# An encoder layer with expert retrieval: one-hot vectors made by ScalarE, rows moved between stages, gate loads from another queue

## The chip, the cores and the metric

The kernel runs on one core of a Trainium2 chip. The metric is the time of one execution on the device, in microseconds. Five engines work beside each other, each through its own list of instructions in order: TensorE (PE in the profile), VectorE (DVE), ScalarE (ACT), GpSimd (POOL) and SyncE (SP, which only issues transfers). They meet at semaphores. Everything is fp32.

## The reference

One layer of an encoder over 512 tokens of width 2048: a mixing part, a cross-attention into 256 memory tokens, and a feed-forward part by retrieval, each with a residual and a LayerNorm. The change touches the last part, and where its work is put beside the two others:

```
q = (xt @ w_pq).reshape(T, PEER_HEADS, PEER_QUERY)
s1 = einsum('thd,nd->thn', q[..., :PEER_HALF], sub_keys1)      # 128 keys
s2 = einsum('thd,nd->thn', q[..., PEER_HALF:], sub_keys2)      # 128 keys
v1, i1 = top_k(s1, 16);  v2, i2 = top_k(s2, 16)
top_s, pos = top_k(all 256 sums v1 + v2, 16);  idx = i1 * 128 + i2 of the chosen
gate = softmax(top_s)
act = gelu(sum over d of peer_u[idx] * x) * gate               # 8 heads x 16 experts a token
out = sum over the chosen experts of act * peer_v[idx]
```

There are 16384 experts, each one row of `peer_u` and one of `peer_v`, of 2048 numbers.

## The kernel before

The 512 tokens are four blocks of 128. Blocks 0 and 1 compute the retrieval **by rows**: for each of 128 chosen places of a token GpSimd gathers one row of `peer_u` for every token of the block (1.05 MB for 128 tokens, an indirect DMA), VectorE takes the dot product (L1898), ScalarE the GELU of four such columns, and VectorE adds the gathered row of `peer_v` times its factor (L1909). One such step for 128 tokens is called a row here; there are 256, each with two transfers of 1.05 MB. The dot product of row k + 4 is done together with the addition of row k. Blocks 2 and 3 (d in the names) compute it **densely**: all 16384 experts in 128 tiles of 128, by TensorE: `U` tiles (L1143), a GELU (L1442), a product with a matrix of gates (`weigh`, L1961), and `V` products (L1170), in four groups of 40, 32, 32 and 24 tiles. Each tile of weights is one transfer of 1 MB from SyncE, with four buffers (`SLOTS`).

The matrix of gates is made in the **one-hot stage**, beside U tiles 19 to 34. A chosen expert is a pair of key numbers. For four tokens at a time (n = 0 to 63) `one_hot_vectors(n)` on VectorE compares the key numbers of the 128 chosen places with the column numbers `IOTA`: plain vectors (is_equal, one TENSOR_TENSOR of 128x512, L1947) and vectors times the gate (four TENSOR_SCALAR, L1950). Their product on TensorE (`one_hots(n)`, L1155, four matmuls of 128x128) is the token's 128x128 matrix of gates. `OH` holds two sets. TensorE does one-hots for two n, half a U tile, two n, the other half. ScalarE copies each result from PSUM (four banks, `stage_gates(n)`) into a staging buffer `WS` for eight n; SyncE stores it to DRAM (`store_gates`), and at the next n divisible by 8 ScalarE waits for that store (`gates_out`) before it overwrites `WS`. Later the gates are loaded back by expert tile (`load_gates(q)`), into two buffers `WD`; q = 0 to 4 by SyncE, from 5 on by GpSimd.

The order of rows is written out by hand: `some_rows(n)` does n rows on VectorE at that place in its list, `HALVES_BEFORE` is how many pairs of rows are done before the V products, and `half_pos` spreads the rest evenly over the 216 positions of the dense part. In the stages of mixing and attention VectorE adds each product of TensorE to x (`add_mix`, L1802), and TensorE waits for these additions and for the norms (L1606 to L1612) behind them before it transposes the result (`turned`, L912). Rows between them on VectorE delay both.

## Time and profile before

| | |
|---|---|
| Three runs | 3187.04, 3189.92, 3194.26 us; median 3189.92 |
| Profiled execution | 3188.36 us, span 3186.5, mean granted TensorE clock 0.989 |
| TensorE busy | 3082.0 us, 97% |
| VectorE busy | 2062.2 us, 65% |
| ScalarE busy | 364.4 us, 11% |
| GpSimd busy | 696.4 us, 22% |
| DMA | 1023.44 MB, mean 321 GB/s |

The page cuts the span into 40 slices of 80 us; each digit is the busy share in tenths, and PEclk the granted clock in tenths.

```profile
PE   8999999999996999999989999999999999999997
DVE  5364633442777798999996766656566565555575
ACT  1223202311001211112210000000000000000000
PEclk9999999999997999999999999999999999999998
DMA  7222221176896698999999999999999999999995
```

TensorE is busy nearly all the time, with one deep slice, the 13th (960 to 1040 us), and VectorE is full around slices 15 to 21. The one-hot stage lies from 1449 to 1620 us, the V products begin at 1668. A share of busy time does not tell what sets the end; the waits and the order of time do.

### The profile page before, as it was taken

The page shows a single profiled execution, that of the slowest core. Times are in us where ns is not written, and L with a number is a line of the kernel's source. Part 1 is how long each engine was busy: PE and PEld are TensorE (multiplying, and loading weights), DVE is VectorE, ACT ScalarE, POOL GpSimd, SP SyncE. Part 2 cuts the span into 40 slices and gives each one's busy share as a digit, 9 for nine tenths or more (in the row PEclk, how much of TensorE's full clock was granted, in tenths as well). Part 3 has the DMA queues.
Part 4 walks back from the last instruction along what each step waited for, and adds up shares of the span by engine and source line. Part 5 has one row for each costly group of instructions (what it writes and reads, how often), then busy time and mean ns, then how long its engine had stood idle before and what let it go on. Part 6 is the DMA issues. An engine that isn't in the chain of part 4 may idle for free.

```text
span 3186.5 us, 26888 instructions
## 1 busy us (share of the span) xinstructions
PE 3082.0 (97%) x10342; PEld 1885.6 (59%) x10342; DVE 2062.2 (65%) x3070; ACT 364.4 (11%) x650; POOL 696.4 (22%) x553
## 2 busy tenths in 40 slices
PE   8999999999996999999989999999999999999997
PEld 5444444444445478679873446885448884468743
DVE  5364633442777798999996766656566565555575
ACT  1223202311001211112210000000000000000000
POOL 0000000000331143422224343223222222222230
PEclk9999999999997999999999999999999999999998
DMA  7222221176896698999999999999999999999995
GB/s 276 73 79 72 82 66 60 37 265 237 317 411 278 259 387 353 422 394 370 380 359 384 399 392 421 421 418 417 418 421 421 418 419 416 422 421 421 418 406 217
DMA packets 151655, 1023.44 MB, mean 321 GB/s; under 512 B 16368, under 2 KB 21616, under 8 KB 35568
## 3 DMA queue, kind: packets, MB, share of 16 engines
q0 software_dynamic: 78800, 559.97, 42.9%
q1 hardware_dynamic: 72736, 461.86, 37.0%
q8 instruction: 78, 1.28, 0.2%
q14 instruction: 41, 0.34, 0.0%
HBM read 1000.79 MB, written 20.97 MB: 321 GB/s over the span
## 4 chain that ended last, share of the span: by engine, by line
DMA 39%; PE 36%; DVE 18%; issue 4%; POOL 1%; ACT 1%; DVEq 0%; SPq 0%; ACTq 0%
DMA arena<-peer_v,arena 37%; PE ps L726 11%; DVE arena L1909 6%; PE ps L1170 5%; PE ps L996 3%; PE ps L1143 3%; PE ps L894 2%; PE ps L920 2%; DVE arena L1950 2%; DVE arena L1898 2%; PE ps L797 1%; DVE arena L1947 1%; DVE arena L1836 1%; DMA arena<-peer_ut 1%; PE ps L690 1%
## 5 line engine op out<-in xcount | busy, mean ns | idle before, releaser
L1170 PE MATMUL ps<-arena 128*128 128x512 f32 x2048 | 884.1, 594 | 18.4 <-DVE arena L1961 14.2
L1143 PE MATMUL ps<-arena 128*128 128x256 f32 x4096 | 892.6, 379 | 2.4 <-DMA arena<-peer_ut 2.4
L1143 PEld LDWEIGHTS ps<-arena 128*128 128x128 f32 x4096 | 774.6, 190 | 110.5 <-DMA arena<-peer_ut 4.6
L1909 DVE SCALAR_TENSOR_TENSOR arena<-arena 128x2048 f32<-128x2048 f32 x256 | 602.9, 2355 | 296.3 <-DMA arena<-peer_v,arena 229.6
L1898 DVE CUSTOM_DVE_ANT_0 arena<-arena 128x2048 f32<-128x2048 f32 x256 | 587.0, 2294 | 276.6 <-DMA arena<-peer_u,arena 275.9
L1170 PEld LDWEIGHTS ps<-arena 128*128 128x128 f32 x2048 | 390.1, 191 | 510.1 <-issue 488.4
L638 POOL DMA_INDIRECT arena<-peer_u,arena x256 | 347.5, 1357 | 1060.9 <-DVE arena L1898 864.5
L653 POOL DMA_INDIRECT arena<-peer_v,arena x256 | 325.5, 1272 | 722.9 <-DVE arena L1909 682.4
L726 PE MATMUL ps<-arena 128*128 128x512 f32 x800 | 345.2, 592 | 1.1 <-ACT arena L1210 1.1
L726 PEld LDWEIGHTS ps<-arena 128*128 128x128 f32 x800 | 151.9, 190 | 192.2 <-issue 192.2
L1210 ACT ACTIVATE arena<-ps 128x512 f32<-128x512 f32 (+2 forms) x247 | 144.5, 612 | 763.6 <-PE ps L912 147.4
L894 PE MATMUL ps<-arena 128*128 128x512 f32 x512 | 221.2, 592 | 0.0
L1424 ACT ACTIVATE arena<-arena 128x4 f32<-128x4 f32 x64 | 13.1, 205 | 1505.7 <-DVE arena L1898 1505.7
L894 PEld LDWEIGHTS ps<-arena 128*128 128x128 f32 x512 | 97.0, 190 | 120.1 <-issue 120.1
L920 PE MATMUL ps<-arena 128*128 128x512 f32 x320 | 139.4, 593 | 2.5 <-ACT arena L1210 2.5
L996 PE MATMUL ps<-arena 128*128 128x256 f32 x640 | 139.6, 380 | 1.2 <-ACT arena L1210 0.8
L996 PEld LDWEIGHTS ps<-arena 128*128 128x128 f32 x640 | 121.4, 190 | 18.5 <-DMA arena<-w_feat 1.2
L920 PEld LDWEIGHTS ps<-arena 128*128 128x128 f32 x320 | 60.5, 190 | 75.3 <-issue 71.8
L1833 DVE MAX8 arena<-arena 128x8 f32<-128x128 f32 (+1 forms) x192 | 52.1, 328 | 43.8 <-ACT arena L1210 38.2
L1674 DVE TENSOR_TENSOR arena<-arena 128x512 f32<-128x512 f32 x16 | 11.0, 689 | 99.9 <-ACT arena L1259 99.9
L1950 DVE TENSOR_SCALAR arena<-arena 128x128 f32<-128x128 f32 x256 | 74.5, 401 | 0.0
L1760 DVE TENSOR_REDUCE arena<-ps 128x1 f32<-128x512 f32 x32 | 22.1, 689 | 72.5 <-PE ps L833 72.0
(183 smaller groups left out, 1847.9 us busy)
## 6 DMA issues: line engine op xcount, KB each, us to landing
arena<-peer_ut SPq DMA_DIRECT2D x128, 1024.0 KB, 9.2
arena<-peer_vt SPq DMA_DIRECT2D x128, 1024.0 KB, 9.1
arena<-w_row SPq DMA_DIRECT2D x52, 1024.0 KB, 8.3
arena<-w_mix SPq DMA_DIRECT2D x40, 1024.0 KB, 4.9
arena<-w_once SPq DMA_DIRECT2D x74, 512.0 KB, 3.5
arena<-w_feat SPq DMA_DIRECT2D x20, 1024.0 KB, 10.0
dense_gates<-arena SPq DMA_DIRECT2D x8, 2048.0 KB, 8.6
arena<-dense_gates POOLq DMA_DIRECT2D x11, 1024.0 KB, 24.5
```

Source lines behind the costliest of these rows:

```text
L638: pool.indirect_dma_start(UB[e], None, peer_u, bass.IndirectOffsetOnAxis(ap=IDX[:, r:r + 1], axis=0)).then_inc(u_full[e], 16)
L653: pool.indirect_dma_start(VB[e], None, peer_v, bass.IndirectOffsetOnAxis(ap=IDX[:, r:r + 1], axis=0)).then_inc(v_full[e], 16)
L726: last = pe.matmul(out_ap, tile(t + half)[:, k * P:(k + 1) * P], A[:, kt * S:(kt + 1) * S], start=(kt == 0), stop=(kt == KT - 1))
L894: last = pe.matmul(bank(k), Y[:, b * D + kt * P:b * D + (kt + 1) * P], w[:, i * 512:(i + 1) * 512], start=(kt == NL), stop=(kt == NL - 1))
L920: last = pe.matmul(bank(k), XT[:, kt * P:(kt + 1) * P], w[:, i * 512:(i + 1) * 512], start=(kt == 0), stop=(kt == KT - 1))
L996: last = pe.matmul(ps[:, k + f // 2, (f % 2) * DT:(f % 2 + 1) * DT], w[:, kt * P:(kt + 1) * P], XTD[:, kt * DT:(kt + 1) * DT], start=(kt = ...
L1143: last = pe.matmul(ps[:, (e // 2) % 4, (e % 2) * DT:(e % 2 + 1) * DT], w[:, kt * P:(kt + 1) * P], XTD[:, kt * DT:(kt + 1) * DT], start=(kt ...
L1170: last = pe.matmul(bank(4 + (c % 2) * 2 + tb), G[:, t * DT + tb * P:t * DT + (tb + 1) * P], w[:, i * 512:(i + 1) * 512], start=(t == 0), s ...
L1210: return act.activation(dst, src, ACT.Copy)
L1898: dve.tensor_tensor_reduce(UB[e], UB[e], xrow(b), 1.0, 0.0, ALU.mult, ALU.add, DOT[r // 4 % 2][:, r % 4:r % 4 + 1]).then_inc(u_free, 1)
L1909: dve.scalar_tensor_tensor(out=acc, in0=VB[e], scalar=AV[r // 4 % 2][:, r % 4:r % 4 + 1], in1=acc, op0=ALU.mult, op1=ALU.add).then_inc(v_f ...
L1950: last = dve.tensor_scalar(oh[:, 0, i], IOTA, turn[:, 0, 4 * n + i:4 * n + i + 1], turn[:, 2, 4 * n + i:4 * n + i + 1], ALU.is_equal, ALU. ...
```

## The change

Five edits. (1) The plain vectors move to ScalarE: `plain_vectors(n)` makes |IOTA - key| with Abs in four ACTIVATE of 128x128 (bias is a column of `TB`), and max(0, 1 - that) with Relu in one of 128x512, which is 1 where the numbers are equal and 0 elsewhere. It uses one buffer `FAR`, and the second step waits for the first. On ScalarE, `plain_vectors(n + 1)` stands ahead of `stage_gates(n)`. TensorE waits for both kinds. (2) In the one-hot stage VectorE does 24 whole rows instead of 16, behind the vectors 1, 4 and 6 of each eight. (3) Ahead of it: twice 4 rows for 6, once 4 for 2. With the 8 more in the stage this is 6 more rows before the V products, `HALVES_BEFORE` 41 for 38. (4) The last store of gates is split, and the first load waits for its first part and the earlier stores only. (5) Gate loads 2, 3 and 4 are issued by ScalarE, between its GELUs, not by SyncE.

```diff
-HALVES_BEFORE = 38
+HALVES_BEFORE = 41
-GELU_AT = [16 * k + 8 for k in range(4)]
+HOT_ROWS = [8 * (i // 3) + (1, 4, 6)[i % 3] for i in range(24)]
+GELU_AT = [HOT_ROWS[4 * k + 3] + 1 for k in range(5)]
+        FAR = OT
 # SyncE
             def load_gates(q):
-                if q >= 2:
-                    sp.wait_ge(g_ready, q - 1)
             def store_gates(k):
                 sp.wait_ge(ws_ev, 8 * k + 8)
-                sp.dma_start(gates_d[k], WS).then_inc(gates_out, 16)
+                if k < DT // TG - 1:
+                    sp.dma_start(gates_d[k], WS).then_inc(gates_out, 16)
+                else:
+                    first = 8 * TG
+                    sp.dma_start(gates_d[k][:, 0:first], WS[:, 0:first]).then_inc(gates_first, 16)
+                    sp.dma_start(gates_d[k][:, first:], WS[:, first:]).then_inc(gates_out, 16)
...
                         if k == DT // TG - 1:
+                            sp.wait_ge(gates_first, 16)
+                            sp.wait_ge(gates_out, 16 * (DT // TG - 1))
+                            load_gates(0)
                             sp.wait_ge(gates_out, 16 * (DT // TG))
-                            load_gates(0)
                             load_gates(1)
-                if p == TILES[0] + 3:
-                    load_gates(2)
...
 # TensorE
                     pe.wait_ge(hots_ready, n + 1)
+                    pe.wait_ge(plain_ready, n + 1)
 # ScalarE
+            def plain_vectors(n):
+                if n >= 2:
+                    act.wait_ge(oh_mm, n - 1)
+                if n:
+                    act.wait_ge(plain_ready, n)
+                for i in range(4):
+                    t = DT + 4 * n + i
+                    last = act.activation(FAR[:, i * NK:(i + 1) * NK], IOTA, ACT.Abs, scale=-1.0, bias=TB[:, t:t + 1])
+                last.then_inc(far_done, 1)
+                act.wait_ge(far_done, n + 1)
+                act.activation(OH[n % 2][:, 4 * NK:8 * NK], FAR, ACT.Relu, scale=-1.0, bias=ONES[:, 0:1]
+                               ).then_inc(plain_ready, 1)
...
+            act.wait_ge(tb_ev, 1)
+            plain_vectors(0)
             for n in range(DT // 4):
+                if n + 1 < DT // 4:
+                    plain_vectors(n + 1)
                 if n % 8 == 1:
                     gelu_dense(0, t)
...
+            def load_gates(q):
+                act.wait_ge(g_ready, q - 1)
+                act.dma_start(WD[q % 2] ...).then_inc(wd_in[q % 2], 16)
...
                 for _ in range(TILES[g]):
+                    if p in (1, 2, 4):
+                        load_gates({1: 2, 2: 3, 4: 4}[p])
                     rows_until(p)
 # VectorE
-                dve.tensor_tensor(oh[:, 1], IOTA.unsqueeze(1).broadcast_to([P, 4, NK]),
-                                  turn[:, 1, here].unsqueeze(2).broadcast_to([P, 4, NK]), ALU.is_equal)
...
                 add_mix(b, 2, k, "mix231.2")
-            some_rows(6)
+            some_rows(4)
...
                 add_mix(b, 0, 6 + k, "mix31.0")
-            some_rows(6)
+            some_rows(4)
...
             best_pairs(0, 2)
-            some_rows(2)
+            some_rows(4)
...
                 one_hot_vectors(n)
-                if n % 4 == 1:
-                    row_ahead(rows[0])
-                if n % 4 == 3:
-                    row_add(rows[0])
-                    rows[0] += 1
+                if n in HOT_ROWS:
+                    some_rows(1)
```

VectorE between the additions of `mix31.0` and `mix31.1` (SCALAR_TENSOR_TENSOR with ps; ISA on 128x2048 is the dot product, the SCALAR_TENSOR_TENSOR on 128x2048 the addition of a row), before:

```order
L1909 SCALAR_TENSOR_TENSOR arena<-arena 128x2048 [waits v_free,v_full4]
L1898 ISA arena<-arena 128x2048 [waits u_full0]
L1898 ISA arena 128x1
L1909 SCALAR_TENSOR_TENSOR arena<-arena 128x2048 [waits v_free,v_full0]
L1921 TENSOR_TENSOR arena<-arena 128x4 [waits gel_done]
L1898 ISA arena<-arena 128x2048 [waits u_full1]
L1898 ISA arena 128x1
L1909 SCALAR_TENSOR_TENSOR arena<-arena 128x2048 [waits v_free,v_full1,act_done]
L1898 ISA arena<-arena 128x2048 [waits u_full0]
L1898 ISA arena 128x1
L1909 SCALAR_TENSOR_TENSOR arena<-arena 128x2048 [waits v_free,v_full0]
L1802 SCALAR_TENSOR_TENSOR arena<-arena,ps 128x512 [waits wb_used] x2
```

And after, where the block has four rows instead of six:

```order
L1938 SCALAR_TENSOR_TENSOR arena<-arena 128x2048 [waits v_free,v_full4]
L1950 TENSOR_TENSOR arena<-arena 128x4 [waits gel_done]
L1927 ISA arena<-arena 128x2048 [waits u_full1]
L1927 ISA arena 128x1
L1938 SCALAR_TENSOR_TENSOR arena<-arena 128x2048 [waits v_free,v_full0,act_done]
L1927 ISA arena<-arena 128x2048 [waits u_full0]
L1927 ISA arena 128x1
L1938 SCALAR_TENSOR_TENSOR arena<-arena 128x2048 [waits v_free,v_full1]
L1831 SCALAR_TENSOR_TENSOR arena<-arena,ps 128x512 [waits wb_used] x2
```

The two rows that stood last before the addition have gone from here; BN_STATS, the norm of block 3, follows it at once in both.

ScalarE in the one-hot stage, before (128x128x4 is the staging copy, 128x512 at L1442 the dense GELU, 128x4 the GELU of four rows):

```order
L1210 ACTIVATE arena<-ps 128x128x4 [waits v_free,u_free,oh_mm]
L1442 ACTIVATE arena<-ps 128x512 [waits wb_used]
L1210 ACTIVATE arena<-ps 128x128x4 [waits oh_mm] x7
L1424 ACTIVATE arena<-arena 128x4 [waits act_done,u_free]
L1210 ACTIVATE arena<-ps 128x128x4 [waits gates_out,oh_mm]
L1442 ACTIVATE arena<-ps 128x512 [waits wb_used]
L1210 ACTIVATE arena<-ps 128x128x4 [waits oh_mm] x7
```

And after, over the first turn of `WS` (128x128 at L1439 is Abs, 128x512 at L1442 Relu, 128x512 at L1459 the dense GELU):

```order
L1214 ACTIVATE arena<-ps 128x128x4 [waits oh_mm]
L1439 ACTIVATE arena<-arena 128x128 [waits plain_ready,oh_mm]
L1439 ACTIVATE arena<-arena 128x128 x3
L1442 ACTIVATE arena<-arena 128x512 [waits far_done]
L1214 ACTIVATE arena<-ps 128x128x4 [waits gates_out,oh_mm]
L1439 ACTIVATE arena<-arena 128x128 [waits plain_ready,oh_mm]
L1439 ACTIVATE arena<-arena 128x128 x3
L1442 ACTIVATE arena<-arena 128x512 [waits far_done]
L1459 ACTIVATE arena<-ps 128x512 [waits wb_used]
L1214 ACTIVATE arena<-ps 128x128x4 [waits oh_mm]
L1439 ACTIVATE arena<-arena 128x128 [waits plain_ready,oh_mm]
L1439 ACTIVATE arena<-arena 128x128 x3
```

Between two copies now stand five instructions and two waits of ScalarE for itself, and those for n + 2 stand behind the copy that waits for `gates_out`.

SyncE at the end of the one-hot stage, before:

```order
L538 DMA dense_gates<-arena 128x4096 [waits ws_ev]
L532 DMA arena<-dense_gates 128x8x256 [waits gates_out]
L532 DMA arena<-dense_gates 128x8x256
L488 DMA arena<-peer_ut 128x2048 [waits wb_used] x2
L488 DMA arena<-peer_vt 128x2048 [waits wb_used] x4
L532 DMA arena<-dense_gates 128x8x256 [waits g_ready]
L488 DMA arena<-peer_vt 128x2048 [waits wb_used]
L532 DMA arena<-dense_gates 128x8x256 [waits g_ready]
L488 DMA arena<-peer_vt 128x2048 [waits wb_used] x2
L532 DMA arena<-dense_gates 128x8x256 [waits g_ready]
L488 DMA arena<-peer_vt 128x2048 [waits wb_used] x33
```

And after; the three loads of gates are now in ScalarE's list:

```order
L544 DMA dense_gates<-arena 128x256 [waits ws_ev]
L545 DMA dense_gates<-arena 128x3840
L534 DMA arena<-dense_gates 128x8x256 [waits gates_out,gates_first]
L534 DMA arena<-dense_gates 128x8x256 [waits gates_out]
L492 DMA arena<-peer_ut 128x2048 [waits wb_used] x2
L492 DMA arena<-peer_vt 128x2048 [waits wb_used] x40
```

## Rows read from the trace of the kernel before

**Rows 1.** Waits of TensorE, whole span: us in total, times, longest.
```profile
PE ps L912 <- DVE arena L1802: 22.7, 1, 22.7
PE ps L1170 <- DVE arena L1961: 14.2, 3, 9.7
PE ps L912 <- DVE arena L1612: 8.6, 4, 5.9
...
PE ps L1170 <- DMA arena<-peer_vt: 4.2, 1, 4.2
```

**Rows 2.** Busy time of stretches; behind it TensorE clock, DMA share, GB/s.
```profile
982.00:993.00 11.00, 4.53 (x20) 4.13 (x20) 10.27 (x24) 2.99 (x5) 0.93 (x1) 0.50 0.98 409
1449.20:1620.00 170.80, 170.54 (x1011) 153.48 (x1010) 169.71 (x360) 40.13 (x76) 45.61 (x31) 1.00 0.96 373
1750.00:3000.00 1250.00, 1250.00 (x4310) 818.70 (x4309) 768.50 (x654) 37.44 (x88) 344.17 (x312) 1.00 1.01 416
```

**Rows 3.** Order of time, TensorE, 946 to 997: start, us, what [idle before].
```profile
946.36 13.90 PE L920 MATMUL ps<-arena 128*128 128x512 f32 x32
982.94 4.53 PE L912 MATMUL ps<-arena 128*128 128x128 f32 x20 [22.68 <-DVE arena L1802]
993.38 3.68 PE L912 MATMUL ps<-arena 128*128 128x128 f32 x16 [5.92 <-DVE arena L1612]
```

**Rows 4.** Order of time, VectorE, 896 to 983.
```profile
896.03 2.35 DVE L1909 SCALAR_TENSOR_TENSOR arena<-arena 128x2048 f32<-128x2048 f32 x1 [0.49 <-DMA arena<-peer_v,arena]
...
914.47 1.88 DVE L1802 SCALAR_TENSOR_TENSOR arena<-arena,ps 128x512 f32<-128x512 f32 x3
...
963.44 2.35 DVE L1909 SCALAR_TENSOR_TENSOR arena<-arena 128x2048 f32<-128x2048 f32 x1 [2.67 <-DMA arena<-peer_v,arena]
...
981.61 1.27 DVE L1802 SCALAR_TENSOR_TENSOR arena<-arena,ps 128x512 f32<-128x512 f32 x2
```

**Rows 5.** Order of time, VectorE (`d.prob`) and TensorE (its transposes), 1035 to 1045.
```profile
1035.59 1.23 DVE L1826 TENSOR_TENSOR arena<-arena 128x1024 f32<-128x1024 f32 x1
...
1043.62 1.04 PE L1012 MATMUL ps<-arena 128*128 128x128 f32 x8
```

**Rows 6.** Order of time, VectorE in the one-hot stage.
```profile
1490.44 0.72 DVE L1947 TENSOR_TENSOR arena<-arena 128x512 f32<-128x512 f32 x1
1491.04 1.15 DVE L1950 TENSOR_SCALAR arena<-arena 128x128 f32<-128x128 f32 x4
1492.06 2.33 DVE L1898 CUSTOM_DVE_ANT_0 arena<-arena 128x2048 f32<-128x2048 f32 x1
```

**Rows 7.** Order of time, TensorE in the one-hot stage.
```profile
1454.44 1.95 PE L1155 MATMUL ps<-arena 128*128 128x128 f32 x16
1456.22 3.62 PE L1143 MATMUL ps<-arena 128*128 128x256 f32 x16
1459.68 1.95 PE L1155 MATMUL ps<-arena 128*128 128x128 f32 x16
```

**Rows 8.** ScalarE by line and form: count, busy us, mean ns.
```profile
L1424 ACT ACT_TABLE_LOAD x14 | 18.0, 1283 | 0.3
...
L1424 ACT ACTIVATE arena<-arena 128x4 f32<-128x4 f32 x64 | 13.1, 205 | 1505.7 <-DVE arena L1898 1505.7
L1255 ACT ACTIVATE arena<-arena 128x512 f32<-128x512 f32 x16 | 10.7, 713 | 1.7 <-ACT arena L1249 1.7
```

**Rows 9.** Order of time, ScalarE, 123 to 128 and 1509 to 1519.
```profile
126.35 1.33 ACT L1255 ACTIVATE arena<-arena 128x512 f32<-128x512 f32 x2 [0.21 <-ACT arena L1249]
...
1517.93 0.60 ACT L1210 ACTIVATE arena<-ps 128x512 f32<-128x512 f32 x1 [7.35 <-DMA dense_gates<-arena]
```

**Rows 10.** Waits of all engines, 1440 to 1640.
```profile
ACT arena L1210 <- DMA dense_gates<-arena: 59.1, 7, 9.7
```

**Rows 11.** Order of time, VectorE and SyncE at the first V products.
```profile
1677.07 0.43 SPq L532 DMA_DIRECT2D arena<-dense_gates  x1
...
1704.44 2.29 DVE L1961 TENSOR_TENSOR arena<-arena 128x2048 f32<-128x2048 f32 x1 [11.73 <-DMA arena<-dense_gates]
```

More of the change, by code:

```diff
@@ L435, in build @@
         hots_ready, oh_mm = sem("hots_ready"), sem("oh_mm")
+        far_done, plain_ready = sem("far_done"), sem("plain_ready")
         ws_ev, gates_out = sem("ws_ev"), sem("gates_out")
+        gates_first = sem("gates_first")
         wd_in = [sem(f"wd_in{e}") for e in range(2)]
@@ L1467, in _ @@
             gelu_rows()
-            gelu_rows()
             pq(0, 2)
@@ L1475, in _ @@
             did(evict(QTD, two_banks(6)), "d.q")
+            gelu_rows()
             gate_exps(2)
@@ L1570, in rows_until @@
                     gate_exps(12 + ROUTE_POS[p])
+            def load_gates(q):
+                act.wait_ge(g_ready, q - 1)
+                act.dma_start(WD[q % 2].rearrange("p (g n) -> p g n", g=DT // TG),
+                              gates_d[:, :, q * 8 * TG:(q + 1) * 8 * TG].rearrange("g p n -> p g n")
+                              ).then_inc(wd_in[q % 2], 16)
             p = 0
@@ L1944, in one_hot_vectors @@
                 oh = OH[n % 2].rearrange("p (a t n) -> p a t n", a=2, t=4)
-                here = slice(4 * n, 4 * n + 4)
                 turn = TB.rearrange("p (a t) -> p a t", a=3)
-                dve.tensor_tensor(oh[:, 1], IOTA.unsqueeze(1).broadcast_to([P, 4, NK]),
-                                  turn[:, 1, here].unsqueeze(2).broadcast_to([P, 4, NK]), ALU.is_equal)
                 for i in range(4):
```

4 lines of the change are left out of this document (removed).

## The prediction

> **What bounds the kernel now.** I read the waits of TensorE first, then busy time by stretches, then the order of time at the places where TensorE stood still. From 1750 to 3000 us TensorE is busy without a gap, the granted clock is 1.00 (2.4 GHz) and the DMA engines move 416 GB/s at a share of 1.01 [rows 2]. The reader is to see that both are full there, but no wait in that stretch is TensorE's: the list of its waits [rows 1] has its large entries elsewhere. So a row taken out of that stretch gives DMA room and no time. What can be won or lost is (a) the 22.7 and 5.9 us before the transposes of L912, (b) the pace of the one-hot stage, 1449 to 1620, (c) the 14.2 and 4.2 us at the start of the V products, L1170.
>
> **Ahead of the one-hot stage.** TensorE ends `b0.pq2` at 946.36 + 13.90 = 960.3 and stands until 982.9, then again 5.9 us until 993.4; the half clock there also makes the two groups of transposes longer [rows 3]. It waits for VectorE's `mix31.1` additions at 981.61, and for the norm behind them [rows 4]. VectorE is late because it does 6 rows before them. Two rows less in the first `some_rows(6)`: the fourth addition of a row ends at 896.03 + 2.35 = 898.4 instead of the start of the additions at 914.47, 16.1 us earlier. `mix31.0` would then be added near 920; with two rows less in the second block, its fourth row, which ended at 963.44 + 2.35 = 965.8, ends 16.1 earlier, at 949.7, 11 us ahead of TensorE's 960.3. The norm of block 3 took 981.61 to 993.38 and now ends near 961.5; TensorE needs it 2.4 us behind 960.3. Both waits go: the second half of the transposes starts at 962.9 instead of 993.4 (30.5), and 1.8 us with it, since the 16 instructions that took 3.68 us ran at a granted clock of 0.50 (1.2 GHz, [rows 2]) and take half at the full one: -32.
>
> The two rows put back behind `best_pairs(0, 2)` come before `d.max0`. Before, `d.prob0` was done at 1036.8 and TensorE wanted it at 1043.6 [rows 5], 6.8 us of cover. Two rows cost 9 us where they lie ready (2.33 and 2.35, [rows 4, 6]) and 16 where both wait for their transfers (the 16.1 above): 2 to 9 us late. I take +3, near the lower end, since this stretch moves little data beside. Part (a): -29, between -33 and -20.
>
> **The one-hot stage.** VectorE, before: per group of four vectors 0.60 us for the plain ones (one TENSOR_TENSOR, 1490.44 to 1491.04) and 1.02 for the weighted ones, and one row of about 4.5 in four groups [rows 6]: 8 n take 8 x 1.63 + 2 x 4.5 = 22.0 us. TensorE alone would take four periods of 5.24 = 21.0 [rows 7]. After: 8 x 1.02 + 3 x 4.5 = 21.7. VectorE is not relieved, it has taken rows for the 8 x 0.60. If nothing else were on the path the stage would be unchanged.
>
> ScalarE now is on the path. One set of plain vectors is four ACTIVATE of 128x128 with a bias column, a wait for their end, and one of 128x512. 128x4 takes 0.205 us; 128x512 with a column operand 0.713; a dependent instruction starts 0.21 behind the end [rows 8, 9]. Between the two ends I place 128x128 at 0.39 and 0.29 from start to start: 1.27 + 0.21 + 0.62 = 2.1 us. With 0.5 for the staging copy that is 2.6 us for each n, against TensorE's 21.0/8 = 2.62: no slack at all. And one wait cannot be hidden: at each n divisible by 8 `stage_gates` waits for the store of the last eight, 59.1 us in 7 times, 8.4 each, up to 9.7 [rows 10]. In the kernel before, nobody queued behind it but copies, and four PSUM banks covered them. Now `plain_vectors(n + 1)` lies ahead of that wait, `plain_vectors(n + 2)` behind it.
>
> One group of eight by hand, t = 0 at the end of one-hots 7: the copy of 7 ends at 0.6, later by 1.7 when set 8 was made between (steady state: 2.3). The wait ends at 2.3 + 8.4 = 10.7; copy 0.5, set 10 at 13.3. TensorE has done one-hots 8 and 9 and its half tile by 1.8 + 2 x 3.46 = 8.7 [rows 7] and stands 4.6 us. Dense GELU, copy 9 and set 11 take 0.5 + 0.5 + 2.1 = 3.1, TensorE's one-hots 10 take 0.9: 2.2 more. VectorE's vectors 12 need one-hots 10 (14.2), then row, vectors, row, vectors: 15.2, 19.8, 20.8, and after one-hots 12 at 21.7: 22.7, 27.2, 28.3, where TensorE wants the last at 27.0: 1.3. Sum 21.0 + 4.6 + 2.2 + 1.3 = 29.1 us for 22.0. Seven such groups and 1 us in the first: +51.
>
> Bounds. Low: a group moves one store of 2.1 MB, two tiles and three rows each of u and v of 1.05 MB, 10.5 MB; at 416 GB/s [rows 2] 25.2 us, where before it was 8.4 MB in 22.0: +26 for eight groups. High: a wait of 9.7 and sets of 2.4 us give 9.7 us a group and +69. I keep +51: 29.1 us is above the DMA's floor, so by this sum the queues do not set it.
>
> The Trainium skill, page "ScalarE: Activation LUTs", section "Rules for kernel authors", advises VectorE, not ScalarE, for Relu and such simple operations. The rows bear it out, 0.60 against 2.1 us. By durations alone the rule says nothing of the sum, since ScalarE is busy 40 of 171 us; it decides only as ScalarE becomes the path. The same page, section "Table sets: the hidden batching unit", has Relu and Abs in every table set; were it otherwise, each set of plain vectors beside a GELU would bring loads of 1.28 us [rows 8]. No run here shows it yet.
>
> **The start of the V products.** VectorE reaches `weigh(0)` by the same work behind the last vectors, but no row addition stands between them and `best_keys(12)`: 2.3 us less [rows 4]. The third gate load waited in SyncE's queue: issued 1677.07, landed at 1704.4, and VectorE stood 11.7 us for it [rows 11]. In ScalarE's queue it is issued behind the GELU of position 1, near the same time, but with no weights ahead of it, and SyncE's weight loads do not stop for `g_ready`. The fourth load comes later than before, behind the GELU of position 3. Of 4.2 and 3.5 us I count 5 won: -7 with the 2.3, between -14 (all but the first wait) and +4 (the last load late by 8 us instead). The split last store gives the first load some microseconds that VectorE does not need. Six rows less behind this point: 0, by [rows 2].
>
> **Sum.** -29 + 51 - 7 = +15. The profiled execution took 3188.4 us (span 3186.5 and 1.9 around it): 3203.4. It lies 1.6 under the median of the runs, so 3205 is forecast.
>
> **Rivals.** (1) The other sign: the stage runs at the DMA's floor, 25.2 us a group. That needs the store's wait below some 5 us, so that set 10 comes at 8.7 with TensorE; for it speaks that SyncE issues the store at once and TensorE's slower pace leaves the queues emptier, against it that the wait was never under 7.35 [rows 9] and rows are added. -29 + 26 - 7 = -10: 3180. Its extreme, ScalarE quite hidden, gives 3190 - 36 = 3154. (2) The chain on ScalarE is longer than 2.1 us a set, or the store takes over 10 us with three rows beside it: +69 to +75 for the stage, 3225. (3) The stall at L912 only moves, to `d.prob0` and the norms behind it: -12 instead of -29, 3222; against it, 11 us of margin. (4) The change evens out, between (1) and the forecast: a group of 26.9, 3190.
>
> **Chances.** Forecast 0.50, own range 3194 to 3218; (1) 0.20; (2) 0.15; (3) 0.08; (4) 0.07. A measurement of this kernel tells about 0.2% (6 us) from no change, so the bounds are 3183.5 and 3196.3. Faster: most of (1), 0.18. Same: (4), the rest of (1), a little of the forecast, 0.14. Slower 0.68. The range leaves out the extreme of (1) and the end of (2): 3172 to 3232.
>
> **What would show it.** TensorE without the 22.7 us wait and `b0.pq2` to L996 in under 10 us; in the one-hot stage a period of 27 to 31 us for eight n, with TensorE's idle time in front of one-hots 10 and 11 of each group, released by ScalarE's Relu; ScalarE busy for most of the stage; the stage some 50 us longer; less waiting at L1170. The forecast is wrong if one-hots 10 are not late (then rival 1), or if the idle time there is released by peer_u or peer_v rows, which would make it a DMA question.

## The result, and the profile after

| | before | changed |
|---|---|---|
| Median of four runs | 3189.03 us | 3297.57 us |
| Range | 3187.04 to 3194.26 | 3289.15 to 3298.22 |
| Profiled execution; span; clock | 3188.36; 3186.5; 0.989 | 3289.15; 3287.1; 0.977 |

The ratio is 1.033, 95% interval 1.031 to 1.035: slower by 108 us, where 15 were forecast. The direction was right, the size wrong by 92 us. One of the four executions of e2 below took 4687 us at a mean granted clock of 0.65 and is left out of its figures.

The two profiled executions differ by 100.6 us in their spans. TensorE's order of time shows where: ahead of the one-hot stage +0.3 us (the first one-hots start at 1449.53 instead of 1449.20), the one-hot stage 265.5 us instead of 170.5 (+95.0), the start of the V products up to the third time that TensorE resumes them +5, the rest 0. The profiled execution of the changed kernel is the fastest of its four, 8.4 us under the median; where the other three lost these 8 us no trace shows.

These are the longest waits of TensorE in the changed kernel, to be set beside [rows 1] (us in total, times, longest). L1159 is `one_hots`, L1174 the V products, L1214 ScalarE's evictions, L1987 `weigh`:

```profile
PE ps L1159 <- issue: 57.8, 15, 8.2
PE ps L1174 <- DVE arena L1987: 24.7, 3, 15.5
PE ps L982 <- ACT arena L1214: 18.4, 2, 17.8
PE ps L1159 <- DVE arena L1976: 15.6, 9, 3.2
PE ps L1034 <- ACT arena L1214: 11.7, 1, 11.7
PE ps L1015 <- DVE arena L1855: 8.7, 1, 8.7
```

The 22.7 us at L912 are gone, and of the 8.6 us for the norms 2.6 are left (the line is L915 now). In their place stand three waits ahead of the stage: 8.7 us at L1015, which is `d.prob0`, and 17.8 and 11.7 us for evictions by ScalarE, which were nowhere in the forecast. "issue" at L1159 is the wait for the plain vectors, whose releaser the view does not name: TensorE goes on 0.1 us behind the end of a Relu (below).

The whole stage, and 6 us behind one of its stalls. The columns are those of [rows 2], whose last three for the stage were clock 1.00, DMA share 0.96 and 373 GB/s:

```profile
1449.53:1715.04 265.51, 192.08 (x1010) 170.87 (x1008) 172.02 (x329) 155.11 (x386) 88.41 (x48) 0.86 0.78 301
1521.75:1528.00 6.25, 5.41 (x20) 4.88 (x21) 4.16 (x7) 6.18 (x17) 0.57 (x1) 0.50 0.27 115
```

TensorE's busy time grew by 21.5 us for the same matmuls, and the granted clock of the stage fell from 1.00 to 0.86. So 73.4 of the 95 us are idle time and 21.5 are slower work. Below is one group of eight n: first TensorE, then ScalarE and VectorE around its end (start, us, what, [idle before]).

```profile
1487.12 2.05 PE L1159 MATMUL ps<-arena 128*128 128x128 f32 x8 [8.21 <-issue]
1490.01 2.04 PE L1159 MATMUL ps<-arena 128*128 128x128 f32 x8 [0.83 <-issue]
1491.84 4.23 PE L1146 MATMUL ps<-arena 128*128 128x256 f32 x16
...
1503.68 1.16 PE L1159 MATMUL ps<-arena 128*128 128x128 f32 x8 [1.47 <-DVE arena L1976]
...
1509.92 3.62 PE L1146 MATMUL ps<-arena 128*128 128x256 f32 x16
1521.75 2.04 PE L1159 MATMUL ps<-arena 128*128 128x128 f32 x8 [8.22 <-issue]
```

```profile
1506.67 0.72 ACT L1442 ACTIVATE arena<-arena 128x512 f32<-128x512 f32 x1
1519.14 0.60 ACT L1214 ACTIVATE arena<-ps 128x512 f32<-128x512 f32 x1 [11.75 <-DMA dense_gates<-arena]
1519.64 1.26 ACT L1439 ACTIVATE arena<-arena 128x128 f32<-128x128 f32 x4
1520.93 0.72 ACT L1442 ACTIVATE arena<-arena 128x512 f32<-128x512 f32 x1
```

```profile
1523.84 1.12 DVE L1976 TENSOR_SCALAR arena<-arena 128x128 f32<-128x128 f32 x4 [11.23 <-PE ps L1159]
```

ScalarE stands 11.75 us for the store of `WS`. Its next set of plain vectors ends at 1521.65, and TensorE goes on at 1521.75, after 8.22 us. VectorE stands too, since `OH` has two sets, and its rows are not done meanwhile. This group is 34.6 us long: 21.0 us of TensorE's work at full clock, 10.5 us idle (0.83, 1.47, 8.22) and 3.1 us more for the same work. Of these 3.1 the rows show 2.6 behind the stall: each of two sets of one-hots took 2.05 us instead of 1.05, the half tile 4.23 instead of 3.62. There are seven such stalls, of 5.3 to 8.2 us, and the one-hots behind each take 2.04 or 2.05 us.

### The profile page after: what moved, and what is told of

Its sections match the earlier page's. It is cut to its first block, busy times and chain, and to the rows that moved or that the text cites. A ratio compares the mean times of both kernels' runs of the same rounds, so it can differ in the third digit from the quotient of the medians.

```text
span 3287.1 us, 27208 instructions
## 1 busy us (share of the span) xinstructions
PE 3100.9 (94%) x10342; PEld 1902.6 (58%) x10342; DVE 2022.5 (62%) x3006; ACT 483.8 (15%) x970; POOL 754.8 (23%) x553
## 4 chain that ended last, share of the span: by engine, by line
PE 83%; DVE 9%; issue 4%; DMA 2%; ACT 1%; POOL 0%; DVEq 0%; SPq 0%; ACTq 0%
PE ps L1174 25%; PE ps L1146 24%; PE ps L729 10%; PE ps L897 6%; PE ps L999 3%; PE ps L923 3%; PE ps L1159 2%; DVE arena L1938 2%; PE ps L800 1%; DVE arena L1927 1%; DMA arena<-dense_gates 1%; DMA arena<-peer_v,arena 1%; PE ps L693 1%; PE ps L1034 1%; PE ps L854 1%
## 5 line engine op out<-in xcount | busy, mean ns | idle before, releaser
L1174 PE MATMUL ps<-arena 128*128 128x512 f32 x2048 | 883.1, 594 | 24.7 <-DVE arena L1987 24.7
L1146 PEld LDWEIGHTS ps<-arena 128*128 128x128 f32 x4096 | 783.1, 192 | 110.6 <-issue 2.6
L1174 PEld LDWEIGHTS ps<-arena 128*128 128x128 f32 x2048 | 390.1, 191 | 515.6 <-issue 488.6
L641 POOL DMA_INDIRECT arena<-peer_u,arena x256 | 405.0, 1582 | 1222.1 <-DVE arena L1927 1039.3
L729 PEld LDWEIGHTS ps<-arena 128*128 128x128 f32 x800 | 151.9, 190 | 192.1 <-issue 192.1
L1214 ACT ACTIVATE arena<-ps 128x512 f32<-128x512 f32 (+2 forms) x247 | 143.8, 611 | 706.1 <-PE ps L923 127.6
L897 PE MATMUL ps<-arena 128*128 128x512 f32 x512 | 221.2, 592 | 0.0
L897 PEld LDWEIGHTS ps<-arena 128*128 128x128 f32 x512 | 97.0, 190 | 120.1 <-issue 120.1
L1159 PE MATMUL ps<-arena 128*128 128x128 f32 x512 | 80.9, 315 | 73.4 <-issue 57.8
L999 PE MATMUL ps<-arena 128*128 128x256 f32 x640 | 139.4, 380 | 1.4 <-ACT arena L1214 1.1
L999 PEld LDWEIGHTS ps<-arena 128*128 128x128 f32 x640 | 121.1, 190 | 18.9 <-ACT arena L1214 1.5
L1159 PEld LDWEIGHTS ps<-arena 128*128 128x128 f32 x512 | 75.1, 223 | 81.1 <-issue 62.4
L1459 ACT ACTIVATE arena<-ps 128x512 f32<-128x512 f32 x64 | 37.8, 592 | 562.2 <-PE ps L1146 562.2
L923 PEld LDWEIGHTS ps<-arena 128*128 128x128 f32 x320 | 60.4, 190 | 75.5 <-issue 71.0
## 6 DMA issues: line engine op xcount, KB each, us to landing
dense_gates<-arena SPq DMA_DIRECT2D x7, 2048.0 KB, 12.8
```

Source lines behind the costliest of these rows:

```text
L641: pool.indirect_dma_start(UB[e], None, peer_u, bass.IndirectOffsetOnAxis(ap=IDX[:, r:r + 1], axis=0)).then_inc(u_full[e], 16)
L729: last = pe.matmul(out_ap, tile(t + half)[:, k * P:(k + 1) * P], A[:, kt * S:(kt + 1) * S], start=(kt == 0), stop=(kt == KT - 1))
L897: last = pe.matmul(bank(k), Y[:, b * D + kt * P:b * D + (kt + 1) * P], w[:, i * 512:(i + 1) * 512], start=(kt == NL), stop=(kt == NL - 1))
L923: last = pe.matmul(bank(k), XT[:, kt * P:(kt + 1) * P], w[:, i * 512:(i + 1) * 512], start=(kt == 0), stop=(kt == KT - 1))
L999: last = pe.matmul(ps[:, k + f // 2, (f % 2) * DT:(f % 2 + 1) * DT], w[:, kt * P:(kt + 1) * P], XTD[:, kt * DT:(kt + 1) * DT], start=(kt = ...
L1146: last = pe.matmul(ps[:, (e // 2) % 4, (e % 2) * DT:(e % 2 + 1) * DT], w[:, kt * P:(kt + 1) * P], XTD[:, kt * DT:(kt + 1) * DT], start=(kt ...
```

## Experiments

There are eighteen kernels. "Stage" is the time from the first one-hots to the first tile behind the last ones, read from the profiled execution; in the kernel before it is 170.5 us. The time given for a kernel is the median of its runs, and the figures in brackets are the 95% interval of its ratio to before.

**1. The stage: which half of the change.** Plain vectors alone (`plain_vectors` and the waits of the diff, applied to before), and the changed kernel without them:

```diff
 # e1_plain_only: before, and
+                    pe.wait_ge(plain_ready, n + 1)
+                if n + 1 < DT // 4:
+                    plain_vectors(n + 1)
 # e2_vector_plain: changed, but
+                dve.tensor_tensor(oh[:, 1], IOTA..., turn[:, 1, here]..., ALU.is_equal)
```

> The kernel before with one edit: the plain vectors made by ScalarE, as in the changed one; 16 rows in the stage, front and gate loads as before. Theory A (ScalarE's list is the path: its wait for the store of WS stands between two sets of plain vectors, so TensorE runs dry once per eight n): the stage grows by most of the 95 us, to 235 to 255 us (a group of 30 to 32 us instead of 22), the whole to 3255 to 3275 us, with 5 us or more of TensorE idle in front of one-hots 10 of each group. Rival B (eight more rows and their 2.1 MB a transfer pair make the stage long, the plain vectors do not): VectorE is relieved by 0.6 us for each n, the stage is 165 to 185 us and the whole within 10 us of 3189.

> The changed kernel with the plain vectors back on VectorE (one TENSOR_TENSOR for each n); 24 rows in the stage, front and gate loads as changed. Theory A: VectorE has 8 x 1.63 + 3 x 4.5 = 26.5 us for a group of eight n and sets the pace, stage 210 to 220 us, whole 3240 to 3250 us (3297 less 50), ScalarE's wait for the store costs TensorE nothing. Rival B (the rows' transfers beside the stores make it long): the stage stays within 15 us of the 265 us of the changed kernel, whole 3285 to 3300 us.

| | rows | plain vectors by | stage | whole | ratio to before |
|---|---|---|---|---|---|
| e1 | 16 | ScalarE | 221.2 | 3237.9 | 1.016 (1.014 to 1.018) |
| e2 | 24 | VectorE | 218.4 | 3249.1 | 1.019 (1.017 to 1.021) |
| changed | 24 | ScalarE | 265.5 | 3297.6 | 1.033 |

In e1 the stage is 50.7 us longer than before. That is less than the 65 to 85 of theory A, and the whole is below its range too, but rival B is excluded: the plain vectors on ScalarE cost this much with 16 rows. TensorE is idle 35.1 us (28.1 for plain vectors, 7.0 for VectorE) and busy 15.6 us longer. ScalarE's waits for the store are 39.4 us in 7, 5.6 each; those of the changed kernel are 76.6 us, 10.9 each. The stores issued between 1455 and 1700 us in e1, then in the changed kernel (KB each, median us from issue to landing):

```profile
dense_gates<-arena SPq DMA_DIRECT2D x8, 2048.0 KB, 7.5
```

```profile
dense_gates<-arena SPq DMA_DIRECT2D x7, 2048.0 KB, 12.8
```

The other kernels agree: the median is 8.6 us in before (16 rows), 12.2 in e2 and 12.4 in e3 (24 rows).

In e2 the stage is 47.9 us longer, as theory A said, with VectorE busy 208.5 of 218.4 us. ScalarE waits even longer for the stores there, 81.7 us, and it costs TensorE 0.8 us, since only copies stand behind that wait. The two differences add up to 98.6 us and both edits together give 95.0, but that is no proof that the causes are apart: VectorE, which is full in e2, is busy only 172 of 265 us in the changed kernel.

**2. The wait for the store.** The stores read another buffer, so ScalarE never waits (the gates in DRAM are not the reference's). The two parts of the last store are changed in the same way, and SyncE waits for the earlier stores ahead of them; this is left out here:

```diff
-                    sp.dma_start(gates_d[k], WS).then_inc(gates_out, 16)
+                    sp.dma_start(gates_d[k], XTD).then_inc(gates_out, 16)
...
-                elif i == 0:
-                    act.wait_ge(gates_out, 2 * n)
```

> The changed kernel, but the stores of the gates read another buffer than WS (so the gates in DRAM are not those of the reference), and ScalarE does not wait for them. All transfers, rows, sets of plain vectors and copies stay. Theory A: the 8 us before one-hots 10, the 1 to 3 behind it and the half clock that follows them go, a group takes 24 to 28 us instead of 34.6 and the whole is 3235 to 3255 us. Rival B (transfers): the idle time moves to the rows, whole above 3280 us. Rival C (ScalarE's chain of 2.1 us a set is too long by itself, with or without the store): a group of 30 us or more, whole 3265 to 3280 us.

e3 takes 3237.9 us, its stage 209.2: theory A. The stores are as slow as in the changed kernel (12.4 us for 12.8), so it is ScalarE's wait for them that costs the time, not the stores. The next kernel keeps the wait and puts the copies two n behind the plain vectors (`stage_gates(n - 2)`):

> The changed kernel with ScalarE's list in another order: its copies of the gates stand two n behind the plain vectors, so that sets up to m + 3 are made before it waits for the store at m; all else as changed, with the wait and the stores real. Theory A (it is the order, not the wait itself): as without the wait, a group of 26 us, stage 205 to 215 us, whole 3237 to 3250 us. Rival B (the four PSUM banks do not cover a wait of 11 us when they stand two behind): the stall moves to TensorE's wait for a bank, stage above 235 us, whole 3265 us or more.

e6 takes 3279.8 us, its stage 255.5. Theory A fails. The times are those of rival B, but not its reason: TensorE waits 59.6 us for ScalarE's Relu and none for a PSUM bank. This order does not help: a lagging copy makes its store late too, and `OH` holds two sets, so TensorE ran out of one-hots some 5 us after ScalarE began a wait of about 10. The next kernel has a second staging buffer, both of half the size, with real stores:

```diff
-TG = 32
+TG = 16
+        WS = [WS2[:, 0:NK * TG], WS2[:, NK * TG:2 * NK * TG]]
...
-                    act.wait_ge(gates_out, 2 * n)
+                    act.wait_ge(gates_out[k % 2], 16 * (k // 2))
```

> The changed kernel with the staging buffer of the gates as two halves of 16 tokens, stored in turn (16 stores of 1 MB instead of 8 of 2 MB), so that ScalarE waits only for the store before the last; all gates are written and loaded as they must be. Theory A (the stall is ScalarE standing for the store of its only staging buffer, with the next sets of plain vectors behind it in its list): as with the wait left out, a group of eight n of 26 us, stage 205 to 215 us, whole 3232 to 3250 us. Rival B (the stores of half the size and the loads in shorter pieces cost as much as the wait, or the wait stays): stage above 240 us, whole 3270 us or more.

e11 takes 3248.4 us (ratio 1.019, 1.018 to 1.021), its stage 209.4, theory A. The rows of its stage, and of that of e12 below:

```profile
1451.42:1660.87 209.45, 177.72 (x1009) 157.95 (x1008) 172.26 (x329) 154.73 (x386) 77.33 (x48) 0.96 0.96 379
```

```profile
1421.42:1606.44 185.02, 168.81 (x1010) 152.57 (x1008) 154.04 (x317) 154.13 (x386) 73.29 (x40) 1.00 0.99 393
```

So 56 of the 95 us are the wait for the store and what follows from it. ScalarE is as busy as in the changed kernel (155 us). With 24 rows and no stall the plain vectors on ScalarE even give a shorter stage than on VectorE, 209.4 us for the 218.4 of e2.

**3. The other 39 us.** In the stage of e11 TensorE is idle 31.7 us and busy 7.2 us longer than before. These are the waits of TensorE for VectorE and of VectorE for TensorE there (us in total, times, longest):

```profile
PE ps L1162 <- DVE arena L1979: 29.6, 18, 4.6
DVE arena L1979 <- PE ps L1162: 18.2, 15, 3.1
```

VectorE is late with the vectors times the gate though it is idle for 37 us itself: 18.2 for TensorE, 12.4 for gathered rows, 6.0 for a GELU. Either a row stands in the wrong place between the vectors, or the transfers hold the stage up. The next kernel is e11 with the rows at `(1, 3, 5)` instead of `(1, 4, 6)`:

> The changed kernel with the two halves of staging, as the one before it (3248 us, stage 209 us), and one more edit: the three rows of each eight n stand behind the vectors 1, 3 and 5 instead of 1, 4 and 6. Theory A (phase: TensorE does two one-hots, half a tile of 3.5 us, two one-hots; a row of 4.5 us on VectorE between vectors n and n + 1 is covered by the half tile only where n is odd, and costs 1.0 to 1.5 us where it is even; there are 16 such waits, 27 to 30 us with the half clock behind some): stage 180 to 196 us, whole 3220 to 3236 us. Rival B (transfers: 10.5 MB for eight n are 25.2 us at 416 GB/s, 202 us for the stage): stage 203 us or more, whole 3240 us or more.

e15 takes 3239.6 us, 9 less than e11, with runs from 3230 to 3249. This lies between the ranges of both theories. The profiled execution is the slowest of the four, so its stage of 212.5 us is not that of the median, and it settles nothing. By the medians the place of the rows is worth 9 us at most, not the 27 to 30 of theory A. The transfers (DMA share 0.96 to 0.97 at 379 to 385 GB/s) can be a part: the 79 MB of e11's stage would take 191 us at the 416 GB/s of [rows 2], 20 us more than before, which is an estimate. With 20 rows (e12 below) the stage is 14.5 us longer than before, not 39. What the 39 us consist of stays open.

**4. The front.** The next kernel is the changed one with seven GELUs of rows moved to later places in ScalarE's list, one of them so:

```diff
             keys(0, 3)
-            gelu_rows()
             product("d.pv")
             did(evict(OTD, two_banks(4)), "d.pv")
             gate_exps(3)
+            gelu_rows()
```

> The changed kernel with seven GELUs of rows on ScalarE moved behind the evictions that TensorE waits for (d.pv, and the keys, turned queries and dense GELUs ahead of each gate_exps); everything else as changed. Theory A (the 11.7 us before the products of attention and the 17.8 us before b1's transposes are evictions queued on ScalarE behind a GELU that waits for rows): both waits go, the stage starts 25 to 32 us earlier, whole 3265 to 3274 us. Rival B (VectorE is late itself, the waits come back as waits for it): whole within 8 us of 3297.

e7 takes 3268.2 us (1.025, 1.023 to 1.027), theory A: 29.3 us are won, and the stage starts at 1421.9. In the changed kernel ScalarE had:

```profile
1024.20 1.28 ACT L1428 ACT_TABLE_LOAD   x1
1038.02 0.20 ACT L1428 ACTIVATE arena<-arena 128x4 f32<-128x4 f32 x1 [12.53 <-DVE arena L1927]
1038.13 1.00 ACT L1214 ACTIVATE arena<-ps 128x1024 f32<-128x1024 f32 x1
```

The GELU waits 12.5 us for the fourth dot product, and behind it stands the eviction that TensorE waits 11.7 us for. GELU j waits for 4j + 4 dot products; with fewer rows ahead of it in VectorE's list, its fourth lies in the next block of rows. The other such place is 1302.15, where ScalarE waited 26.2 us and TensorE 17.8.

The next kernel has the front's edit alone, on before, and its four rows go to the dense part:

```diff
-HALVES_BEFORE = 38
+HALVES_BEFORE = 36
-            some_rows(6)
+            some_rows(4)    # both blocks, one early gelu_rows() less
```

> The kernel before with one edit ahead of the one-hot stage: each of the two blocks of six rows between the additions of the mixing stage has four, and the four rows go to the dense part (two pairs of halves fewer before the V products), one GELU of rows on ScalarE with them; one-hot stage and gate loads as before. Theory A (the 22.7 and 5.9 us before the transposes were rows in VectorE's way; the changed kernel got nothing from it only since its order of GELUs on ScalarE lost the same again): both waits go, nothing comes in their place, 3155 to 3165 us. Rival B (whatever is moved ahead of the stage is lost further on, since TensorE meets the next late work of VectorE at d.prob0 or of ScalarE at b1): 3180 to 3192 us.

e5 takes 3184.8 us (0.999, 0.998 to 1.000): rival B by its time, but not by its reason. The stage starts 28.1 us earlier (1421.09), and the third time that TensorE resumes the V products comes 27.7 earlier. Nearly all of it is lost at one place, the last V products:

```profile
2993.26 15.70 PE L1170 MATMUL ps<-arena 128*128 128x512 f32 x32 [3.65 <-DVE arena L1960]
3025.54 140.55 PE L1170 MATMUL ps<-arena 128*128 128x512 f32 x320 [16.58 <-DVE arena L1960]
```

Four rows are 8.4 MB, which at the 420 GB/s of that part would be 20 us, an estimate; 26 us are lost between the third resumption and the end. In the dense part, where TensorE and the transfers are both full, six rows taken out gave nothing (the changed kernel), and four put in cost 26 us. TensorE's waits there name `weigh` on VectorE, so that it is the bytes that cost the time, and not VectorE's work on the rows, is not shown.

**5. The start of the V products.** e4 is before with the last two edits alone; e10 is the changed kernel with its gate loads 2 to 4 back in SyncE's queue:

> The kernel before with the last two edits only: the last store of gates split, the first load behind its first part, and gate loads 2 to 4 issued by ScalarE. Stage and front as before. Theory A (load 4, behind ScalarE's GELU of position 3, is asked for late: in the changed kernel and in the two others with this edit the third start of the V products waited 15.5 to 20.8 us, without it 3.5 to 4.5): the waits at the start of the V products are 22 to 28 us in sum instead of 17.5, whole 3193 to 3200 us. Rival B (the late load is a matter of the late stage only): 3180 to 3190 us.

> The changed kernel with gate loads 2 to 4 back in SyncE's queue; everything else as changed, the split last store too. Theory A (in ScalarE's list loads 3 and 4 stand behind GELUs of rows; with 82 rows instead of 76 ahead of the V products the fourth row of a GELU comes two rows later there, so load 4 is issued at 1812 instead of within 25 us of load 2): the 15.5 us wait at the third start of the V products falls to 3 to 5, at the second start it rises by up to 4; whole 3285 to 3293 us. Rival B (the loads are late because of the stage's late stores, not of the queue): 3294 to 3301 us.

e4 takes 3186.7 us (0.999, 0.998 to 1.000), rival B. e10 takes 3284.2 (1.030, 1.029 to 1.032), 13.4 less than the changed kernel and a little below theory A's range. TensorE's three waits at the start of the V products are 6.7, 3.6 and 1.4 us in e10 and 6.7, 2.5 and 15.5 in the changed kernel. The new queue of the loads costs nothing on before, and 13 us together with the other edits. ScalarE's issues in the changed kernel:

```profile
1759.88 0.38 ACTq L1595 DMA_DIRECT2D arena<-dense_gates  x1
...
1768.77 0.20 ACT L1428 ACTIVATE arena<-arena 128x4 f32<-128x4 f32 x1 [7.13 <-DVE arena L1927]
1768.78 0.37 ACTq L1595 DMA_DIRECT2D arena<-dense_gates  x1
1811.93 0.21 ACT L1428 ACTIVATE arena<-arena 128x4 f32<-128x4 f32 x1 [42.95 <-DVE arena L1927]
1811.94 0.37 ACTq L1595 DMA_DIRECT2D arena<-dense_gates  x1
```

The load for q = 4 stands behind a GELU that waits for a fourth row; with 82 rows ahead instead of 76 the fours fall two rows later, and the load is asked for at 1811.9, 52 us behind the first. In e4 the same three are issued at 1666.8 (two) and 1687.9.

**6. Do the losses add up, and is there a better kernel?** The next kernel is the changed one with the GELUs of e7, the stagings of e11 and the loads of e10:

> The changed kernel with three mends together: the GELUs behind the evictions, the two halves of staging, gate loads 2 to 4 back in SyncE's queue; still 24 rows in the stage and four rows fewer in the two blocks. Theory A (the three losses are apart and add up: 29, 50 to 60 and 3 to 8 us of the 3297.6): 3200 to 3215 us. Rival B (the front's gain or the loads' is taken back in the stage, whose 24 rows are bound by VectorE and the transfers): 3220 us or more.

e13 takes 3203.5 us (1.005, 1.003 to 1.007): theory A. The three mends give 29.3, 49.2 and 13.4 us by themselves, 91.9 in sum, and 94.1 together. The other 39 us of the stage are still in e13: its stage takes 211.0 us, but it starts 26.8 us earlier than in before, which pays for most of that. The next two kernels have twenty rows in the stage, four of them from the front, and plain vectors by ScalarE, first with late copies (e8), then with two stagings (e12):

> A version from the findings so far: the kernel before, with the two blocks of six rows ahead of the stage cut to four; the four rows go to the one-hot stage (20 instead of 16, none more in the dense part); there the plain vectors are made by ScalarE with its copies two n behind. Gate loads as before. Theory A (a stage whose ScalarE does not stop needs 21 to 23 us for eight n with 2.5 rows: TensorE 21.0, VectorE 19.4, transfers 9.4 MB at 416 GB/s 22.7; the 30 us that the front gives are lost only where the rows go to the full dense part): stage 172 to 188 us, whole 3160 to 3180 us. Rival B (the gain ahead of the stage is eaten again wherever the rows go): 3185 us or more.

> The kernel before with four rows moved from the two blocks ahead of the stage into it (20 instead of 16), plain vectors by ScalarE right ahead of its copies, and the two halves of staging; gate loads as before. Theory A (VectorE 8 x 1.02 + 2.5 x 4.5 = 19.4 us, TensorE 21.0, transfers 22.7 us for eight n; the front's 30 us stay): stage 172 to 188 us, whole 3162 to 3180 us. Rival B (ScalarE's 2.6 us for each n with no slack, and three waits between engines for each n, keep a group at 25 us or more even so): stage 200 us or more, whole 3190 us or more.

e8 takes 3218.5 us and its stage 232.9. That is rival B by its time but not by its reason: the stage starts at 1421.65, so the front's gain is there, and ScalarE's waits for stores (53.3 us) stall TensorE as in e6. e12 has a stage of 185.0 us as theory A said, but takes 3189.4 us (1.000, 0.999 to 1.001), with single runs from 3179.5 to 3191.7. The profiled execution is the fastest of the ten by 6 us, so the stage of the median may be longer. To see what the two stagings cost by themselves, e14 has them on before alone, and e17 adds a layout in DRAM whose loads read pieces of 1 KB again:

> The kernel before with the two halves of staging only. Theory A (no engine that TensorE needs stands behind the wait there, four PSUM banks cover it): no change, 3183 to 3195 us. Rival B (stores and loads in smaller pieces cost by themselves): 3197 us or more, with longer waits at the start of the V products.

> The kernel before with the two halves of staging (3200 us by themselves) and the same layout in DRAM, so that gate loads read pieces of 1 KB again. Theory A (the 12 us came from loads in pieces of 512 B, in the dense part whose transfers are full): 3183 to 3192 us. Rival B (from VectorE's access to weights in runs of 16 numbers, or from the number of stores): 3196 to 3203 us.

```diff
 # e17, beside e14
+                sp.dma_start(gates_d[k // 2, :, :, k % 2, :], WS[k % 2].rearrange("p (q n) -> p q n", n=8 * TG))
```

e14 takes 3200.1 us (1.003, 1.002 to 1.005), rival B by its time. The waits at the start of the V products, which that rival named, grow by 1.8 us only; the rest is at the last V products (0.95 us in before):

```profile
3003.03 27.63 PE L1173 MATMUL ps<-arena 128*128 128x512 f32 x64
3039.09 140.48 PE L1173 MATMUL ps<-arena 128*128 128x512 f32 x320 [8.43 <-DVE arena L1964]
```

e17 takes 3188.5 us (1.000, 0.999 to 1.001), theory A: loads in pieces of 512 B instead of 1 KB cost 11.6 us. The next kernel is e12 with this layout and with its rows behind odd n:

> The version with 20 rows in the stage, four of them from ahead of it, plain vectors by ScalarE and two halves of staging (3189 us), with the gates laid out in DRAM so that the loads read pieces of 1 KB as before (the stores write pieces of 512 B), and the rows of the stage behind odd n only. Theory A (the halves cost 12 us in the dense part through loads in pieces of 512 B, and rows behind even n some microseconds in the stage): 3168 to 3180 us, faster than both kernels. Rival B (the 12 us are the many small stores or the halves' DVE access, not the pieces of the loads): 3184 to 3192 us.

e16 takes 3203.4 us (1.005, 1.003 to 1.006), and both theories fail: the stage is 212.4 us. ScalarE's waits for stores are 40.7 us instead of 15.3 in e12, so the stores, now in pieces of 512 B, are the likelier cause. e17 and e14 show the same side by side: with the new layout the median time of a store to its landing is 16.4 us instead of 13.6, and ScalarE waits 116.6 us for them instead of 75.7. It costs nothing there, since only copies stand behind the waits. In e16 the layout and the odd rows were not separated.

The last two kernels have only the cut of the two blocks of rows, on before. The four rows stand where VectorE was idle, and two GELUs of ScalarE are moved to later places (e18); e19 has the gate loads too:

```diff
-            some_rows(6)      # both blocks
+            some_rows(4)
                 probs(DPR[...], 1 + tb, f"d.exp{tb}", f"d.prob{tb}")
+            some_rows(2)
             for c in QUAD:
+                if c == 3:
+                    some_rows(2)
```

> The kernel before with its one-hot stage, gate loads and numbers of rows as they were; only four rows stand elsewhere: two from each of the two blocks of six go to where VectorE stood idle (two behind d.prob, where it waits 9.7 us for b0.key3, two ahead of the last additions of d.wo, where it waits 8.5 us for TensorE), with their GELUs on ScalarE behind evictions that TensorE waits for. Theory A (the 22.7 and 5.9 us are rows in VectorE's way; the gain stays if neither the full dense part nor ScalarE's order takes it back): 3158 to 3170 us, faster than both kernels. Rival B (the dense part, whose transfers are full, takes back what comes earlier, as with the four rows put into it): 3178 to 3190 us.

> The same with the last two edits of the change added (last store split, gate loads 2 to 4 from ScalarE's queue, which with 76 rows ahead of the V products cost nothing: 3186.7 us by themselves). Theory A: 3154 to 3168 us, 2 us less than without them. Rival B (earlier weights then meet the loads): up to 8 us more than without them.

e18 takes 3167.0 us (0.993, 0.992 to 0.995), e19 3164.5 (0.993, 0.991 to 0.994): theory A, both faster than before and than the change. TensorE in e18:

```profile
964.93 27.89 PE L996 MATMUL ps<-arena 128*128 128x256 f32 x128 [0.27 <-ACT arena L1210]
...
1038.16 9.28 PE L1031 MATMUL ps<-arena 128*128 128x512 f32 x16 [5.92 <-DVE arena L1808]
1049.51 7.10 PE L1031 MATMUL ps<-arena 128*128 128x512 f32 x16 [2.06 <-DVE arena L1808]
```

L996 starts at 964.9 instead of 998.6; of the 33.6 us won there, 21.5 are left at the start of the stage (1427.71) and 20.4 in the span. The two rows before the last additions of d.wo cost 4.6 (8.0 us of waits at L1031 instead of 3.4), and behind them TensorE waits 4.0 us for a norm. e19 is not told apart from e18.

## Why the prediction was wrong, step by step

In the profiled executions the sum was off by 85 us: 29 ahead of the stage, 44 in it, 12 behind it. The rest of the 92 is that the profiled execution lies further below its median than that of the kernel before.

- **L912 waits go, 32 us: right.** L996 (now L999) started at 964.74, 33.8 us earlier.
- **"`d.prob0` ... I take +3": too small.** The wait at L1015 is 8.73 us, at the upper end of "2 to 9".
- **Part (a) as a whole, -29: failed**, the result is 0. The step left out is ScalarE: I moved rows on VectorE and followed TensorE's waits for VectorE, not the GELUs in ScalarE's list, whose waits count rows. They gave back 11.7 and 17.8 us. e7 shows it: with them moved, the 29 us appear. Rival (3) had the stall move to `d.prob0` and the norms behind it, for -12. Some of it did move there (8.7 us); the greater part went to ScalarE's evictions, which no rival had.
- **The set of plain vectors, 2.1 us: right** (1484.51 to 1487.0 for copy and set). Its length alone did not decide: e3 and e11 have the same chain and lose 39 us, not 95. The Trainium skill, page "ScalarE: Activation LUTs", section "Rules for kernel authors", advises VectorE for Relu. Here that advice held for the changed kernel (e2 takes 3249.1 us, the changed kernel 3297.6) and not where ScalarE has no stall (e11's stage is 209.4 us, e2's 218.4). The same page of the Trainium skill, section "Table sets: the hidden batching unit", has Relu and Abs in every table set, and the trace agrees: there are 310 Abs and Relu between 1449 and 1715, GELUs among them, and no ACT_TABLE_LOAD.
- **The stall: the right mechanism, mis-sized.** Its signs came as written: idle time in front of one-hots 10 and 11, released by ScalarE's Relu. "4.6 before one-hots 10" measured 8.2, "2.2 before 11" 0.8, VectorE's 1.3 measured 1.5. The term that failed was the store's wait: 8.4, "up to 9.7", measured 10.9, up to 11.8. I had bounded it by a stage with 16 rows; with 24 the stores take 12.2 to 12.8 us to land, with 16 they take 7.5 to 8.6, whoever makes the plain vectors. How the rows' transfers delay a store was not looked into.
- **Left out: the clock behind the stall.** In the 6 us behind a stall of 8.2 us the granted clock was 0.50, the one-hots behind all seven stalls took twice their time, and the group shown took 3.1 us more for the same work. [rows 3] had shown the same at L912, and I had used it there.
- These make 34.6 for 29.1 us, seven times: 39 us. The other 5 of the 44 between +51 and +95 are my base: I took 22.0 us for a group before, eight of which are 176 us, where the stage took 170.5.
- **Rival (1)'s floor of +26: too low even where the stall is gone.** e3 and e11 have +39. The stage moves 379 to 381 GB/s there, not the 416 of the dense part.
- **V products, -7: wrong sign, +5.** The first wait fell from 9.7 to 6.7 us. The bound of "+4 (the last load late by 8 us)" named what happened, but too small: 15.5 us of wait instead of 3.5. Of the two counts of rows that were run, 76 did not make the load late (e4) and 82 did; the same edit changed the count. The bound of -14 does not come out of its terms, which are 4.2, 3.5 and 2.3 us.
- **"Six rows less in the dense part: 0": right**, 1452.3 us against 1452.1. The reverse is not free (e5).

## What to carry to other kernels

Moving work on one engine moves the due time of every instruction of other engines that counts it. Go through each of their lists for such waits, and for what is queued behind them. Copies may stand behind an engine's wait for a store: four PSUM banks covered 59 us of such waits in before and 82 in e2. The inputs of TensorE may not, since only two sets of them fit. Where TensorE and the transfers are both full, look for a place where the moved work's engine is idle and the transfers have room: in before VectorE waited 9.7 and 7.2 us between 1038 and 1085, with a DMA share of 0.69 to 0.87 from 1046 to 1080, and four rows moved to places near there gave 22 us (e18).

## What the runs showed of the hardware

- A store of 2.1 MB lands in 7.5 us (median) in a stage with 16 rows and 294 GB/s (e1), and in 12.8 us in one with 24 rows and 301 GB/s (the changed kernel). In before it is 8.6 us at 373 GB/s, in e2 12.2 at 367. The mean traffic did not tell the latency.
- Sixteen loads of 1 MB in pieces of 512 B instead of 1 KB cost 11.6 us of the whole (e14 and e17); it shows mostly as TensorE's wait at the last V products, behind 1240 us with a DMA share of 1.01.
- Behind a stall of 8.2 us the granted clock was 0.50, and TensorE's eight 128x128 matmuls took 2.05 us instead of 1.05. Behind one of 3.4 us the first eight took 1.13 and the next 2.05 (e8).
